# Input tiles scaled by a diagonal matrix while they are turned, and the first norm's weights multiplied into the rows of the input projection

## The reference, cut to what matters

```python
def rms_norm(x, g):
    y = xf * lax.rsqrt(jnp.mean(xf * xf, axis=-1, keepdims=True) + EPS)
    return (y * g).astype(x.dtype)
...
    h = rms_norm(x, ln1)                     # x: rows x 1024, ln1: 1024
    proj = h @ w_in                          # w_in: 1024 x 2568
    q, k, v, f, xr, yg = jnp.split(proj, SPLITS, axis=-1)
    # forgetting attention of q, k, v with logf = log_sigmoid(f + b_f)
    # causal convolution and gated linear recurrence (RG-LRU) of xr, gelu(yg) as its gate
    x = x + mixed @ w_out
    h2 = rms_norm(x, ln2)
    x = x + jnp.square(jax.nn.relu(h2 @ w_up)) @ w_down
```

## Time and profile before

| | us |
|---|---|
| median of 3 runs | 1440.4 (1440.22 to 1440.63) |
| the profiled execution | 1439.09 |
| its span in the profile | 1437.4 |
| PE busy in the span | 1376.5 (96%) |
| DVE / ACT / POOL busy | 1003.8 / 522.7 / 389.7 |
| TensorE's mean granted clock | 0.988 of 2.4 GHz |

### The profile page before, as it was taken

The page is one execution under the profiler, slowest core; times in us unless marked ns, Lnnn a source line. Parts: engine busy times, 40 slices in busy tenths (PEclk is TensorE's granted clock), DMA queues, the critical chain, the costliest instruction groups (busy, mean ns, idle before and its releaser), DMA issues.

```text
span 1437.4 us, 21430 instructions
## 1 busy us (share of the span) xinstructions
PE 1376.5 (96%) x7479; PEld 1172.7 (82%) x7487; DVE 1003.8 (70%) x1523; ACT 522.7 (36%) x964; POOL 389.7 (27%) x396
## 2 busy tenths in 40 slices
PE   5889999999999999899999999999999999999998
PEld 4674955948748887688999999999999999999997
DVE  6654363544633567766788888888888888888885
ACT  5124233242344565332433343334323343334330
POOL 5310111101100002111432553345334543355320
PEclk9899999999999999999999999999999999999999
DMA  6023432414333121212101110111011110121004
GB/s 198 9 70 86 113 88 77 123 49 134 85 96 87 31 90 53 80 47 88 57 3 58 58 58 0 58 58 58 22 36 58 58 51 7 58 58 58 0 29 132
DMA packets 129545, 92.90 MB, mean 65 GB/s; under 512 B 14679, under 2 KB 119127, under 8 KB 129493
## 3 DMA queue, kind: packets, MB, share of 16 engines
q1 hardware_dynamic: 129492, 92.20, 22.5%
HBM read 78.28 MB, written 9.71 MB: 61 GB/s over the span
## 4 chain that ended last, share of the span: by engine, by line
PE 86%; DVE 5%; DMA 4%; ACT 2%; POOL 1%; issue 1%; SPq 1%; DVEq 0%; POOLq 0%
PE psum L2040 16%; PE psum L2041 16%; PE psum L2042 16%; PE psum L2519 8%; PE psum L2521 8%; PE psum L2520 8%; DMA k_c<-in_cache_k_dram 3%; PE psum L2303 2%; PE psum L2254 2%; PE psum L2285 1%; PE psum L2288 1%; PE psum L2313 1%; PE psum L2410 1%; PE psum L2124 1%; DVE tops L1611 1%
## 5 line engine op out<-in xcount | busy, mean ns | idle before, releaser
L1906 DVE TENSOR_TENSOR mix<-mix,psum 128x512 f32<-128x512 f32 x660 | 417.8, 681 | 91.9 <-PE psum L2521 87.5
L2040 PE MATMUL psum<-h_hi,wu_hi 128*128 128x384 f32 x768 | 259.5, 338 | 0.9 <-DVE wu_lo L1871 0.9
L2041 PE MATMUL psum<-h_lo,wu_hi 128*128 128x384 f32 x768 | 258.1, 336 | 0.0
L2042 PE MATMUL psum<-h_hi,wu_lo 128*128 128x384 f32 x768 | 258.1, 336 | 0.0
L2519 PE MATMUL psum<-wd_hi,u_hi 128*128 128x512 f32 x516 | 201.3, 390 | 0.1
L2521 PE MATMUL psum<-wd_hi,u_lo 128*128 128x512 f32 x516 | 200.7, 389 | 0.0
L2520 PE MATMUL psum<-wd_lo,u_hi 128*128 128x512 f32 x516 | 200.7, 389 | 0.0
L2040 PEld LDWEIGHTS psum<-h_hi,wu_hi 128*128 128x128 f32 x768 | 144.3, 188 | 10.0 <-issue 1.3
L2041 PEld LDWEIGHTS psum<-h_lo,wu_hi 128*128 128x128 f32 x768 | 144.3, 188 | 8.7
L2042 PEld LDWEIGHTS psum<-h_hi,wu_lo 128*128 128x128 f32 x768 | 144.4, 188 | 0.0
L1263 ACT CAST wd_hi<-raw 128x512 fp32r<-128x512 f32 x109 | 67.1, 621 | 179.7 <-PE psum L2521 81.2
(11 more groups left out here) (321 smaller groups left out, 2471.6 us busy)
## 6 DMA issues: line engine op xcount, KB each, us to landing
raw<-in_w_up_dram SPq DMA_DIRECT2D x32, 512.0 KB, 6.0
raw<-in_w_down_dram SPq DMA_DIRECT2D x32, 512.0 KB, 4.5
k_c<-in_cache_k_dram SPq DMA_DIRECT2D x32, 256.0 KB, 3.2
raw<-in_w_in_dram SPq DMA_DIRECT2D x32, 192.0 KB, 4.0
out_dram<-mix SPq DMA_DIRECT2D x9, 512.0 KB
v_c<-in_cache_v_dram SPq DMA_DIRECT2D x16, 256.0 KB, 4.3
raw<-in_w_in_dram SPq DMA_DIRECT2D x8, 512.0 KB, 5.9
raw<-in_w_out_dram SPq DMA_DIRECT2D x8, 512.0 KB, 4.2
```

The source lines that it names most:

```text
L1906: nc.vector.tensor_tensor(half_of(t, half), half_of(t, half), psum[:, product_bank(n), :].rearrange("p (k n) -> p k n", n=P), op).then_inc ...
L2040: nc.tensor.matmul(out, hi(k), r_hi(k), start=first and k == 0, stop=False)
L2041: nc.tensor.matmul(out, hi(k), r_lo(k), start=False, stop=False)
L2042: last = nc.tensor.matmul(out, lo(k), r_hi(k), start=False, stop=end and k == n - 1)
```

## The change

- The 128 x 1024 copy `ln1_b` goes. `ln1` comes as 8 x 128 (`ln1_r`, 4 KB instead of 512 KB), PE transposes it first of all, DVE copies it to `ln1_c` (128 x 8).
- `x_norm` goes, nine instructions of DVE. POOL now multiplies the identity by the tile's reciprocal roots (`diag`, 128 x 128, seven buffers), and `turn` is eight plain float32 matmuls of the raw tile with that diagonal instead of eight transposes.
- `ln1` is multiplied into weights: `pair_hi` becomes eight ACT instructions of 384 columns with a scale for each pair, `pair_lo` eight DVE instructions; the forget weights are scaled by one small DVE instruction; and each of the eight blocks of the recurrence's weights is multiplied in place by POOL (`scale_weights`, 128 x 1024) before ACT may read it.
- PE's order: turn(5) and forgets(0) now stand ahead of the small parameters. POOL's constants move behind several `x_rstd_of`. DVE's small steps are in a new order.

```diff
-            sp.dma_start(ln1_b[:], ln1.to_broadcast([P, D])).then_inc(ln1_in, 16)
+            sp.dma_start(ln1_r[:], ln1.rearrange("a (k p) -> (a k) p", p=P)).then_inc(ln1_in, 16)
...
             def x_rstd_of(t):
                 pool.wait_ge(x_mean, t + 1)
-                nc.gpsimd.tensor_tensor(x_rs[:, t:t + 1], x_ms[:, t:t + 1], neg_half[:, 0:1], ALU.pow).then_inc(x_rstd, 1)
-                pool.wait_ge(x_rstd, t + 1)
+                n.link(nc.gpsimd.tensor_tensor(x_rs[:, t:t + 1], x_ms[:, t:t + 1], neg_half[:, 0:1], ALU.pow))
+                if t >= 7:
+                    pool.wait_ge(x_turned, 2 * (t - 7) + 2)
+                nc.gpsimd.tensor_scalar(diag[:, t % 7, :], ident[:], x_rs[:, t:t + 1], None, ALU.mult).then_inc(diag_ready, 1)
+                pool.wait_ge(diag_ready, t + 1)
...
+            def scale_weights(c, u):
+                pool.wait_ge(raw_in[u], RAW_LRU + 16 * c + 16)
+                w = raw[:, u, :].rearrange("p (k n) -> p k n", k=KC)
+                nc.gpsimd.tensor_tensor(w, w, ln1_c[:, :, None].to_broadcast([P, KC, P]), ALU.mult).then_inc(wl_scaled, 1)
+                pool.wait_ge(wl_scaled, 2 * c + u + 1)
...
             def pair_hi(p, j):
                 act.wait_ge(raw_in[j], 32 * p + 32)
-                nc.scalar.copy(wp_hi[:, 2 * j:2 * j + 2, :].rearrange("p k n -> p (k n)"),
-                               raw[:, j, 0:2 * PW3]).then_inc(w_hi, 1)
+                act.wait_ge(ln1_ready, 1)
+                for k in (2 * j, 2 * j + 1):
+                    done = nc.scalar.activation(wp_hi[:, k, :], raw[:, j, (k % 2) * PW3:(k % 2 + 1) * PW3], ACT.Copy,
+                                                scale=ln1_c[:, k:k + 1])
+                done.then_inc(w_hi, 1)
...
             def lru_hi(c, u):
-                act.wait_ge(raw_in[u], RAW_LRU + 16 * c + 16)
+                act.wait_ge(wl_scaled, 2 * c + u + 1)
...
-            def x_norm(t):
-                dve.wait_ge(x_rstd, t + 1)
-                nc.vector.scalar_tensor_tensor(x_at(t), x_at(t), x_rs[:, t:t + 1], ln1_b[:],
-                                               ALU.mult, ALU.mult).then_inc(x_normed, 1)
...
             def turn(t):
-                pe.wait_ge(x_normed, t + 1)
+                pe.wait_ge(diag_ready, t + 1)
                 if t >= 2:
                     pe.wait_ge(h_lo_ready, 2 * (t - 2) + 2)
                 for b in range(2):
                     for k in range(4):
-                        last = nc.tensor.transpose(psum[:, x_bank(t) + b, k * P:(k + 1) * P],
-                                                   x_at(t)[:, (4 * b + k) * P:(4 * b + k + 1) * P], ident[:])
+                        last = nc.tensor.matmul(psum[:, x_bank(t) + b, k * P:(k + 1) * P],
+                                                x_at(t)[:, (4 * b + k) * P:(4 * b + k + 1) * P], diag[:, t % 7, :],
+                                                start=True, stop=True)
                     last.then_inc(x_turned, 1)
```

More of the change, by code:

```diff
@@ L868, in _ @@
                     pair_rstd(p, t)
+            def scale_weights(c, u):
[3 more added lines that the diff above has]
+                pool.wait_ge(wl_scaled, 2 * c + u + 1)
+            for u in range(2):
+                scale_weights(0, u)
             pool.wait_ge(st_done, STEPS * PAIRS)
@@ L872, in _ @@
             nc.gpsimd.memset(xpad[:, 0:3], 0.0).then_inc(gates_free, 1)
+            for c in range(1, LC):
+                for u in range(2):
+                    scale_weights(c, u)
             pool.wait_ge(proj_done, 6 * LC)
@@ L1414, in first_stage @@
                 if i == 0:
[L1415 to L1427 removed]
+                    dve.wait_ge(rows_turned, 1)
@@ new lines, in first_stage @@
+                    nc.vector.tensor_copy(ln1_c[:], psum[:, 5, 0:KC]).then_inc(ln1_ready, 1)
+                    x_mean_of(0)
+                    x_mean_of(1)
+                    turn_lo(0)
+                    x_mean_of(2)
+                    turn_lo(1)
+                    dve.wait_ge(ln1_ready, 1)
+                    for j in range(4):
+                        pair_lo(0, j)
+                    x_mean_of(3)
+                    turn_lo(2)
+                    dve.wait_ge(wf_in, 16)
+                    nc.vector.tensor_tensor(wf_raw[:], wf_raw[:], ln1_c[:, :, None].to_broadcast([P, KC, H]),
+                                            ALU.mult).then_inc(ln1_ready, 1)
@@ L1436, in first_stage @@
[L1436 to L1441 removed]
+                    turn_lo(6)
                     past_sums()
@@ L2067, in first_stage @@
                     turn(4)
+                    turn(5)
+                    forgets(0)
                     pe.wait_ge(small_in, 16 * SMALL)
@@ L2072, in first_stage @@
                     last.then_inc(rows_turned, 1)
-                    turn(5)
-                    forgets(0)
                     turn(6)
```

74 lines of the change are left out of this document (36 added, 38 removed).

## The result

The changed kernel takes **1448.25 us** (median of five, 1446.19 to 1450.01), the kernel before 1440.22 beside it: a ratio of **1.0061, 95% interval 1.0046 to 1.0076**. The forecast was 1441.4 with a range up to 1447; the kernel is slower, by more than the range allows. The profiled execution has a span of 1448.0 us, 10.6 more than the one of before.

The account below looks back on a forecast made before the run. TensorE (PE) was taken to bound the kernel, 86% of what ended last, so edits count where PE waits. Front -4.0, pairs +0.7, chunk 3's stall +2.3 and clock +2.0 sum to +1.0 on 1440.4: 1441.4 us, range 1436 to 1447.

Parts of the forecast that it names:

- front: First stage: PE freed from waits for DVE's `x_norm` and `h_lo`, with forgets(2)'s clock; -4.0 us, between 0 and -5.4.
- pairs' weights in halves: Pairs' weights: `pair_hi` parts become two scaled ACT instructions of 384 columns, partly exposed in pairs 1 to 3; +0.7 us.
- POOL's multiplications and the clock behind them: Recurrence, chunk 3: uncovered scaling delays ACT's first gate read, +2.3 us; half clock behind PE's gap, +2.0 us.
- The other edits: 0: Small `ln1` transposition and copy, forget-weight scaling and later `param` on DVE stand in gaps of their engines; 0 us.
- Start, up to project(0): 0: Kernel start: dropped `ln1` copy and norm against longer turns at half clock; taken as 0, bounds 1 us either way.
- From 22.8 us to forgets(2): -3.3: First stage: forgets(0) starts at 28 or so, forgets(2) at 41.9 instead of 45.21, with PE at full clock; -3.3 us.
- The clock of forgets(2): End of the first stage's forgets: 5.1 us at half clock, 2.9 or 3.0 at full; a third taken, -0.7 us.
- Six of the eight are covered: POOL's multiplications for chunks 0 to 2 finish before ACT wants them; only chunk 3 has no cover.
- The clock behind the gap, +2.0: PE's 3.0 us gap before chunk 2's third gate matmul brings half clock behind it; +2.0 us, bounds none and 3.4.
- the likeliest case: Rival 1, the forecast: front gives 2.5 to 5 us, chunk 3 takes back 3 to 6; 1438 to 1445, chance 0.52.
- Rival 4: First-stage turns: a plain turn costs four transposes, 4.1 us; +11 us on the forecast, 1452, chance 0.04.
- Rival 3: First stage: front gives nothing, clock falls after project(0) as before; +5.0 us, 1445.4, or 1447 with dearer POOL; chance 0.23.

Follow-up runs that it names:

- two mirror kernels: Changed kernel with `ln1_c` in spare columns, nothing behind shifted: 1443.39 us, 1.0031; kernel before with 32 unused bytes in front of `h_keep`: 1444.65 us, 1.0035.
- front_alone: Changed kernel's first stage alone, at the addresses of the kernel before, pairs' and recurrence's weights not multiplied by `ln1`: 1436.10 us, 0.9989.
- recurrence_part_alone: Kernel before plus POOL's eight multiplications of the recurrence's weights, by a column of ones, ahead of ACT's rounding: 1443.47 us, 1.0031.
- shift64: Kernel before with 64 unused bytes a partition in front of `h_keep`, so every tile behind lies 64 bytes later: 1.0049.
- recurrence_behind_qk: Kernel before with POOL's eight multiplications by ones, chunk 0's waiting until DVE's last product of queries, keys and gain has run: 1442.81 us, 1.0032.
- candidate3: Changed kernel at the addresses of before, chunk 0's multiplications behind `qk_ready`, chunk 3's weights issued early, POOL's memsets ahead of tile 3's root: 1435.59 us, 0.9972.
- pairs_part_alone: Kernel before with `pair_hi` and `pair_lo` in halves of 384 columns, a column of ones as scale: 1.0008, +1.2 us.

## Why the prediction was wrong, step by step

| step | forecast, us | measured alone, us |
|---|---|---|
| front | -4.0 (0 to -5.4) | -1.6 (-3.3 to +0.1) |
| pairs' weights in halves | +0.7 (0 to +3) | +1.2 (-0.1 to +2.3) |
| POOL's multiplications and the clock behind them | +4.3 (0 to +7) | +4.5 (+2.6 to +6.5) |
| addresses of the tiles | not a term | +5.0 (+3.3 to +6.9) |
| sum | +1.0 | +9.1; the whole kernel +8.8 |

**What failed first: a term that was not there.** The last step of the sum, "The other edits: 0", counted instructions. `ln1_c` was taken for a copy in a gap of DVE; I did not look at where its 32 bytes move the tiles behind it, and no row of the kernel before could have priced that. Without it the changed kernel stands at 1.0031, 1444.9 on the scale of the forecast, inside the range and at the forecast's upper edge. The two mirror kernels show this; it is the cause of the miss. Of the 8.1 us between +1.0 and +9.1, it is 5.0, the front 2.4.

**Front: the right size came out of the wrong place, and a piece was left out.** "Start, up to project(0): 0" was wrong for the profiled execution: turn(3) starts at 20.99 us against 22.83, -1.8, and 1.4 us of it fall into project(0), since the granted clock is at full level from 10.2 us on and not from 20.2. It is no accident of one execution: in the ten traces with the new front full level begins at 10.2 to 13.0 us, in the ten with the old one at 18.7 to 21.5. "From 22.8 us to forgets(2): -3.3" came out as +0.2 (22.55 us from turn(3) to forgets(2) against 22.38). I had put forgets(0) 5.5 us behind turn(3); it is 8.4. Of these 2.9 us, 2.6 are the two waits for the diagonals that POOL makes behind its memsets: I had costed the diagonal (0.5, measured 0.61) and the turn (1.85, measured 1.95 to 2.05 with the last one's tail), and had not walked POOL's queue between them. With the memsets moved the stretch is 3.0 shorter than before, near the forecast. A reading was wrong too: the 3.9 us of gaps "ahead of the fall" are those of the whole stretch to 30.9 us, and the clock fell at 27.0. Only some 1.6 us of them lie ahead of the fall, so the argument that gaps of under 1 us would hold the clock had less behind it than it seemed. "The clock of forgets(2)", -0.7, was -1.0. That the front as a whole is worth 1.6 by the medians where its stage shows 3.3 lies inside the interval. Half a us of the rest shows in front_alone's trace: PE comes earlier to chunk 3 and waits 1.21 us there and not 0.71. Whether falls of the clock in later stages eat a part is open.

**Pairs.** Mechanism and size hold. The halves take 1.11 us a pair of them (forecast 1.03 to 1.1), and exponential 10 to 14 of pair 0 takes 5.90 us, from 117.37 to 123.27, where the earlier trace rows has 5.63.

**POOL's multiplications.** The chain of numbers at chunk 3 was met nearly to the digit: first rounding at 520.13 (forecast 520.0), second at 523.62 (523.6), gate read at 524.55 (524.5), PE's gap 3.31 (3.0). That it was met so closely is luck: POOL's instruction is shorter than assumed (1.90 and not 2.4), and it starts later (518.20 and not 517.5), which cancel. "Six of the eight are covered" was wrong: ACT indeed waits for none of them, but the first of them held up DVE at 383 us, worth 1.3 us of PE's time in the profiled execution and a stretch at half clock. The prediction asked who waits for POOL and not who runs beside it.

**The clock behind the gap, +2.0.** The stretch of 3.4 us at half clock came as forecast. But it does not go by the length of this gap alone: 2.93 us in recurrence_part_alone brought it (at 526.2 us), and so did 1.96 us in shift64; 3.02 us in recurrence_behind_qk did not. A term of half its price, with both ends kept, was the right way to treat it.

**The rivals.** The mechanism of the likeliest case happened at chunk 3, with the term for addresses on top and less from the front. Rival 4 is excluded: a turn of plain matmuls takes 1.95 to 2.05 us against 1.03 of transposes, a factor of 1.9 (from its start to the start of what follows without a gap, 1.8 against 0.80 to 0.88, a factor of 2.0 to 2.3). The Trainium skill, TensorE: Matmul & The Clock Gate, section Terms, gives four for float32; for this use the measurement decides. Rival 3 did not come: there is no half clock between 22.8 and 44.3 us.

## What to carry to other kernels

Before an edit is costed, compare the addresses of all tiles in the two builds: a small allocation in the middle of a stack can cost more than the edit's instructions, and putting it into spare columns leaves everything where it was. When work is put on a queue that looks idle, walk that queue for what now stands behind it (the diagonals behind the memsets), and look which engine reads beside it (DVE's product), not only who waits for its result. A piece that has no cover, as chunk 3's weights, is better fetched earlier than made cheaper.

## What the runs showed of the hardware

- The pitch of back-to-back matmuls depends on where their tiles lie in a partition, at full clock, with no gap: 173.3 to 176.7 ns for 384 columns, 226.6 to 234.2 ns for 512, in the MLP each value the same to about 0.1 ns wherever the same addresses were used. The MLP of this kernel takes 655.2 us for 14 blocks at its first place, 662.2 when moved by 32 or 64 bytes, 665.8 by 128. What the matmul waits for in there no run tells.
- A DVE instruction of eight columns took 1.86 us in place of 0.16 beside POOL's multiplication; DVE's `cross_qk`, with one 64 x 512 input in PSUM and one in SBUF, took its usual 0.74 us at 385.77 us in candidate3, while POOL multiplied from 382.93 to 386.80.
- ACT takes 0.31 us for a piece of 128 columns with a scale, back to back (2.45 us for eight), 0.56 for 384 with a scale and 1.05 for 1024 in one plain instruction: a fixed cost of some 0.2 us each, as an estimate from the three.
- Where the clock falls and for how long differs from trace to trace. Behind the first stage it stood at half for 10 to 34 us in the twenty profiled executions, which moves a time by 12 us at most. It is most of the scatter of single runs: in the 34 executions of the kernel before that stand beside pairs_part_alone, the mean granted clock lies between 0.984 and 0.993, and the time goes with it (correlation -0.87). A step of a few us in one pair of traces needs the medians beside it.
- A gap of PE of 1.96 to 3.31 us ahead of chunk 3 brought a stretch of 3.4 us at half clock in four traces; gaps of 2.52 and 3.02 us at the same place, in two others, brought none there.
